# Output projections and the first dense chunks of a decoder trunk: two weight chunks begun together, four row tiles in PSUM banks 4 to 7, their last two inner slices at the end

## The chip, the cores and the metric

The kernel runs on one core of one Trainium2 chip. The metric is the time of the whole program in microseconds of device time; lower is better. Times in this text are microseconds unless marked otherwise.

TensorE (PE) multiplies into PSUM, which has eight banks; VectorE (DVE) and ScalarE (ACT) read PSUM and SBUF, GpSimd (POOL) reads SBUF; SyncE (SP) issues the weight DMAs. Each engine works through its own list in order and meets the others at semaphores.

## What is computed

One inference step of a decoder trunk of two layers, in fp32, for a prompt of 256 tokens and 8 sample tokens with the same weights (264 token columns together), D_MODEL = 1024:

```
for i in range(DEPTH):
    mix = mixer(rms_norm(x, norm_mix_g[i]), ...)      # z = xn @ w_in; conv, retention, gates
                                                      # m = sigmoid(ga)*a + sigmoid(gr)*r;  mix = m @ w_o
    x = x + mix
    hn = rms_norm(x, norm_ffn_g[i])
    if i % 2 == 0:
        f = swiglu(hn, w_dense_gu, w_dense_down)      # layer 0: dense, inner width 3584
    else:
        f = moe(hn, w_router, w_exp_gu, w_exp_down)   # layer 1: top 2 of 8 experts
    x = x + f
    gate = sigmoid(rms_norm(x, norm_ple_g[i]) @ w_ple_gate[i])
    x = x + gate * (p[i] @ w_ple[i])
return rms_norm(x, norm_final_g), conv states, retention states
```

The change touches m @ w_o in both layers and the first columns of hn @ w_dense_gu in layer 0.

## The kernel before

**Tiles and chunks.** Activations lie transposed: a row tile is 128 features by 264 tokens, and x has eight of them. Weights stream in chunks of 128 by 2048 fp32 (1 MB). SP loads chunk c into `raw`, a ring of six. ACT rounds it to `whi` (`cast`, L994) and DVE writes the remainder to `wlo` (`cast`, L1537), both rings of three. A product is three matmuls, whi x hi, whi x lo, wlo x hi (`three`, L2135). A chunk of the output projection or the dense up projection holds eight inner slices (k = 0 to 7) of two row tiles, so a row tile is 24 matmuls and a chunk 48.

**Order and waits.** ACT may cast chunk c once chunk c - 2 has begun on PE (`chunk_begun`, given by the first matmul of a chunk). PE waits for `lo_done` of its chunk (`ready`). A finished row tile gives `tile_ready`; the engine that reads it out gives `tile_taken`. Tiles are numbered through the program; tile p goes to bank p % 3 and waits until tile p - 3 is taken, unless `IN_BANK` and `FREE_AFTER` (L400 to L409) name another bank and another tile to wait for (`free`, L2126). `chunk` (L2143) runs its row tiles one after the other, all eight slices of each; with `each` the first tile waits before every slice for that slice's right operand.

**Output projection ("o", four chunks, eight row tiles, both layers).** Its right operand is m, in frt, split into high and low parts tile by tile; the low parts are DVE's L1734, and the tiles of x that the result is added to are DVE's L1763. The first chunk is run by `chunk_late` (L2160): six slices of tile 0, six of tile 1, then the last two slices of tile 0 and of tile 1; its two tiles are in banks 4 and 5. The other three chunks go through `chunk`. DVE's list in this stage is, for i = 0 to 3:

```
for i in range(4):
    cast(b["o"] + i + AHEAD)                     # AHEAD = 2
    if i > 0: split_x(..., 2 * i - 1)            # xl of tile 2i-1
    for j in (2 * i, 2 * i + 1): ...             # L1763: x[:, j] += PSUM, gives tile_taken
    split_x(..., 2 * i)                          # xl of tile 2i
```

ACT's list runs alike: cast of chunk o+i+2, then the high parts of x (`split_x`, L1001) for tiles 2i-1 and 2i, each waiting for DVE's add. POOL sums the squares of the x tiles into `sacc` as they come (`squares`, L585).

**Dense block, first half ("gu0", layer 0).** Right behind o. Its first chunk takes xh and xl as right operands, slice k waiting for xl of x tile k. After the first three slices of its second tile come two matmuls (`stat`, "L2282") that sum `sacc` over the partitions; from them ACT takes a root (L1019) and DVE makes rstd (`recip`, L1559), with which DVE multiplies every gu0 tile as it drains it (`take`, L1568, in rows L1571). ACT's list here: cast gu0+2, root, wait for the drains of tiles 0 and 1, Silu of both, cast gu0+3. DVE's: cast gu0+2, rstd, drain tiles 0 and 1, cast gu0+3, drain tiles 2 and 3, cast gu0+4 and so on.

**Behind o in layer 1** come the first tile of the w_ple product, then matmuls with an identity that turn xh and xl into token rows (`token_hi`, `token_lo`, L1832 and L1838), and the routing. The third `token_lo` writes the bank of o's last tile and waits for `tile_taken` of all o tiles.

**The input projection of layer 1** already starts with `two_late` (L2182): two chunks together, six slices of each of four tiles, stat, then the last two slices of all four.

Of the kernel before, what the change touches and what calls it, by code (L numbers as in the profile page):

```python
# [44 lines left out]
DEPTH = 2  # L45
# [5 lines left out]
RAW, CAST = 6, 3  # L51
# [99 lines left out]
def program(nc, A, O):  # L151
# [4 lines left out]
    with es:  # L156
# [247 lines left out]
        IN_BANK.update({TB[l]["o"] + i: 4 + i for l in range(DEPTH) for i in range(2)})  # L404
# [4 lines left out]
        FREE_AFTER.update({TB[l]["o"] + i: None for l in range(DEPTH) for i in range(2)})  # L409
# [1709 lines left out]
        def _(pe):  # L2119
            mm = nc.tensor.matmul  # L2120

            def ready(c, turns=0):

                pe.wait_ge(lo_done, RAW * turns + c + 1)
# [35 lines left out]
            def chunk_late(c, p, each, norm, ah, al):  # L2160

                ready(c)
                outs = [free(p), free(p + 1)]

                def some(n, ks):

                    for k in ks:
                        if n == 0:
                            pe.wait_ge(each[0], each[1][k])
                        at = k * 256 + n * 128  # L2170
                        ins = three(outs[n], whi[:, c % CAST, at:at + 128], wlo[:, c % CAST, at:at + 128],
                                    ah[:, k, :], al[:, k, :], k == 0, k == 7, n == 0 and k == 0)
                    return ins

                some(0, range(6))
                some(1, range(6))
                some(0, (6, 7)).then_inc(tile_ready, 1)
                if norm is not None:
                    stat(norm)
                some(1, (6, 7)).then_inc(tile_ready, 1)  # L2180

            def two_late(c, p, each, norm):  # L2182

                outs = [free(p + n) for n in range(4)]

                def some(n, ks, begins=False):

                    cc, h = c + n // 2, n % 2
                    for k in ks:
                        if n == 0:  # L2190
                            pe.wait_ge(each[0], each[1][k])
                        at = k * 256 + h * 128
                        ins = three(outs[n], whi[:, cc % CAST, at:at + 128], wlo[:, cc % CAST, at:at + 128],
                                    xht[:, k, :], xlt[:, k, :], k == 0, k == 7, begins and k == ks[0])
                    return ins

                ready(c)
                some(0, range(6), True)
                some(1, range(6))
                ready(c + 1)  # L2200
                some(2, range(6))
                some(3, range(6))
                stat(norm)
                some(0, (6, 7)).then_inc(tile_ready, 1)
                some(1, (6, 7)).then_inc(tile_ready, 1)
                some(2, (6, 7), True).then_inc(tile_ready, 1)
                some(3, (6, 7)).then_inc(tile_ready, 1)
# [101 lines left out]
            for l in range(DEPTH):  # L2309
# [14 lines left out]
                else:  # L2324
                    two_late(b["in"], t["in"], x_split(24), 3)
# [94 lines left out]
                chunk_late(b["o"], t["o"], (m_lo, [8 * l + k + 1 for k in range(8)]), None, frt[:, 8:16, :], frt[:, 16:24, :])  # L2420
                for i in range(1, 4):
                    chunk(b["o"] + i, t["o"] + 2 * i, 8, 2, frt[:, 8:16, :], frt[:, 16:24, :])
                if l == 0:
                    for hf in range(2):
                        c0, t0 = b["ffn"] + 22 * hf, t[f"gu{hf}"]
                        if hf == 0:
                            chunk(c0, t0, 8, 2, xht, xlt, each=x_split(8), norm=1, at_tile=1, at_k=2)
                        else:
                            chunk(c0, t0, 8, 2, xht, xlt)
                        chunk(c0 + 1, t0 + 2, 8, 2, xht, xlt)  # L2430
# [59 lines left out]
```

## Time and profile before

| | |
|---|---|
| median of 3 runs | 1721.24 us (1718.92 to 1721.98) |
| the profiled execution | 1718.33 us, span 1716.5 us |
| PE busy | 1697.8 us (99% of the span) |
| DVE busy | 1398.7 us (81%) |
| ACT busy | 1084.9 us (63%) |
| POOL busy | 188.8 us (11%) |
| DMA | 494.92 MB, mean 288 GB/s |
| mean granted TensorE clock | 0.998 |

The profile is of one execution; its span runs from the first to the last instruction. A matmul's length in a row (0.28 us for 264 columns) holds its way through the array; in a row of matmuls they start every 0.12 us. The time in brackets stands with an instruction in front of which its engine was idle, with the engine and line that ended the idle time.

### The profile page before, as it was taken

Reading aid. Unit: us, or ns where it says so; the run is one execution under the profiler, and the core shown is the slowest. Engines: PE = TensorE matmul, PEld = TensorE weight load, DVE = VectorE, ACT = ScalarE, POOL = GpSimd, SP = SyncE. Lnnn points to the kernel's source line nnn. Section 1 sums busy time; section 2 is a strip of 40 time slices with the busy share of each in tenths; the row PEclk is TensorE's granted clock in tenths of the full one; section 3 lists DMA queues with packets and bytes.
Section 4 is the critical chain, followed back from the end, with each engine's and each line's share of the span. In section 5 each row is a group of like instructions: output and inputs, shape, how many; then the busy total and the mean of one; then the engine's idle time right before and its main releaser. Section 6 shows DMA issues by size and latency. Waiting matters only on the chain.

```text
span 1716.5 us, 27369 instructions
## 1 busy us (share of the span) xinstructions
PE 1697.8 (99%) x10380; PEld 1517.3 (88%) x10380; DVE 1398.7 (81%) x1271; ACT 1084.9 (63%) x922; POOL 188.8 (11%) x166
## 2 busy tenths in 40 slices
PE   9999999999999999999999999999999999999997
PEld 8999999999999999878888888888888888888787
DVE  7876776566697867799898989898888988989898
ACT  5345444434563454677777777777777777777766
POOL 2112410000221122430000000000000000000002
PEclk9999999999999999999999999999999999999999
DMA  9755555655565554599999999999999999999990
GB/s 305 253 185 166 172 173 151 208 179 150 196 197 196 174 178 153 186 356 389 373 393 393 363 392 376 370 394 369 375 388 370 379 390 353 394 384 342 383 358 26
DMA packets 281536, 494.92 MB, mean 288 GB/s; under 512 B 8472, under 2 KB 127464, under 8 KB 281460
## 3 DMA queue, kind: packets, MB, share of 16 engines
q1 hardware_dynamic: 275104, 473.03, 77.2%
q0 software_dynamic: 6144, 20.67, 4.5%
q8 instruction: 55, 0.90, 0.2%
q10 hardware_dynamic: 212, 0.14, 0.0%
q14 instruction: 21, 0.17, 0.0%
HBM read 481.58 MB, written 12.23 MB: 288 GB/s over the span
## 4 chain that ended last, share of the span: by engine, by line
PE 88%; DVE 7%; ACT 2%; DMA 2%; issue 1%; DVEq 0%; POOL 0%; SPq 0%; ACTq 0%
PE PS L1920 11%; PE PS L1924 11%; PE PS L1923 11%; PE PS L2137 11%; PE PS L2140 10%; PE PS L2141 10%; PE PS L1940 6%; PE PS L1944 6%; PE PS L1943 6%; DVE wlo L1540 3%; DMA raw<-in_w_exp_gu 2%; ACT whi L999 2%; PE PS L1958 1%; PE PS L2381 1%; DVE xl L1547 1%
## 5 line engine op out<-in xcount | busy, mean ns | idle before, releaser
L1540 DVE TENSOR_TENSOR wlo<-raw,whi 128x2048 fp32r<-128x2048 f32 x450 | 1039.6, 2314 | 220.6 <-ACT whi L999 215.9
L999 ACT ACTIVATE whi<-raw 128x2048 fp32r<-128x2048 f32 x449 | 860.2, 1918 | 363.8 <-PE PS L2137 158.2
L1920 PE MATMUL PS<-whi,xh 128*128 128x512 f32 x896 | 355.1, 396 | 2.2 <-DVE wlo L1540 1.6
L1924 PE MATMUL PS<-whi,xl 128*128 128x512 f32 x896 | 349.7, 390 | 0.0
L1923 PE MATMUL PS<-wlo,xh 128*128 128x512 f32 x896 | 349.1, 390 | 0.0
L2137 PE MATMUL PS<-xh,whi 128*128 128x264 f32 x1168 | 334.4, 286 | 1.4 <-DVE z L1571 1.0
L2140 PE MATMUL PS<-xl,whi 128*128 128x264 f32 x1168 | 331.0, 283 | 0.0
L2141 PE MATMUL PS<-xh,wlo 128*128 128x264 f32 x1168 | 330.8, 283 | 0.0
L2137 PEld LDWEIGHTS PS<-xh,whi 128*128 128x128 f32 x1168 | 220.0, 188 | 2.8 <-DVE xl L1547 0.9
L2140 PEld LDWEIGHTS PS<-xl,whi 128*128 128x128 f32 x1168 | 220.1, 188 | 0.2
L2141 PEld LDWEIGHTS PS<-xh,wlo 128*128 128x128 f32 x1168 | 219.0, 188 | 0.0
L1920 PEld LDWEIGHTS PS<-whi,xh 128*128 128x128 f32 x896 | 168.4, 188 | 38.3 <-DVE wlo L1540 4.7
L1924 PEld LDWEIGHTS PS<-whi,xl 128*128 128x128 f32 x896 | 168.2, 188 | 35.9
L1923 PEld LDWEIGHTS PS<-wlo,xh 128*128 128x128 f32 x896 | 168.4, 188 | 33.0
L1940 PE MATMUL PS<-whi,fr 128*128 128x512 f32 x448 | 175.4, 391 | 0.1
L1944 PE MATMUL PS<-whi,fr 128*128 128x512 f32 x448 | 174.4, 389 | 0.0
L1943 PE MATMUL PS<-wlo,fr 128*128 128x512 f32 x448 | 174.4, 389 | 0.0
L2137 PE MATMUL PS<-fr,whi 128*128 128x264 f32 x480 | 137.4, 286 | 1.2 <-DVE fr L1734 1.2
L2141 PE MATMUL PS<-fr,wlo 128*128 128x264 f32 x480 | 136.4, 284 | 0.0
L2140 PE MATMUL PS<-fr,whi 128*128 128x264 f32 x480 | 135.9, 283 | 0.0
L1940 PEld LDWEIGHTS PS<-whi,fr 128*128 128x128 f32 x448 | 84.1, 188 | 18.1 <-DVE wlo L1540 0.9
L1944 PEld LDWEIGHTS PS<-whi,fr 128*128 128x128 f32 x448 | 84.1, 188 | 17.5
(322 smaller groups left out, 1674.8 us busy)
## 6 DMA issues: line engine op xcount, KB each, us to landing
raw<-in_w_exp_gu SPq DMA_DIRECT2D x224, 1024.0 KB, 7.3
raw<-in_w_exp_down SPq DMA_DIRECT2D x112, 1024.0 KB, 6.7
raw<-in_w_in SPq DMA_DIRECT2D x43, 1024.0 KB, 5.5
raw<-in_w_dense_gu SPq DMA_DIRECT2D x28, 1024.0 KB, 5.0
raw<-in_w_dense_down SPq DMA_DIRECT2D x16, 896.0 KB, 5.1
raw<-in_w_o SPq DMA_DIRECT2D x8, 1024.0 KB, 4.8
raw<-in_w_ple_gate SPq DMA_DIRECT2D x8, 1024.0 KB, 7.0
scr<-in_state_ret POOLq DMA_DIRECT2D x8, 512.0 KB, 4.8
```

The costliest lines, as they stand in the source:

```text
L999: nc.scalar.activation(whi[:, c % CAST, :], raw[:, c % RAW, :], ACT.Copy).then_inc(hi_done, 1)
L1540: v.tensor_tensor(wlo[:, c % CAST, :], raw[:, c % RAW, :], whi[:, c % CAST, :].bitcast(F32), ALU.subtract).then_inc(lo_done, 1)
L1547: v.scalar_tensor_tensor(lo[:, j, :], x[:, j, :], vec[:, GAIN[norm] + j:GAIN[norm] + j + 1], hi[:, j, :].bitcast(F32), ALU.mult, ALU.subtr ...
L1920: ins = mm(PS[:, bank, :], gh[:, 128 * kk:128 * kk + 128], wh, start=kk == 0, stop=False)
L1923: mm(PS[:, bank, :], gh[:, 128 * kk:128 * kk + 128], wl, start=False, stop=False)
L1924: ins = mm(PS[:, bank, :], gl[:, 128 * kk:128 * kk + 128], wh, start=False, stop=kk == 7)
L1940: ins = mm(PS[:, h, :], ah, wh, start=first and kk == 0, stop=False)
L1943: mm(PS[:, h, :], ah, wl, start=False, stop=False)
L1944: ins = mm(PS[:, h, :], al, wh, start=False, stop=last and kk == 3)
L2137: ins = mm(out, wh, ah, start=first, stop=False)
L2140: mm(out, wh, al, start=False, stop=False)
L2141: return mm(out, wl, ah, start=False, stop=last)
```

## The change

`chunk_late` goes. `two_late` gets the operands and a place for stat as arguments and is used in three more places: the first two chunks of o in both layers, and the first two chunks of gu0. In each, PE does slices 0 to 5 of tiles 0, 1 (first chunk), 2 and 3 (second chunk), and then slices 6 and 7 of tiles 0, 1, 2, 3. The second chunk's `chunk_begun` is given by the first of its last slices. The four tiles lie in banks 4 to 7. In gu0, stat comes after the six slices of the third tile instead of within the second. Tiles 4 to 6 of o wait only for what was before o to be taken; gu0's tiles 0 to 3 wait for o's tiles 0 to 3. Tile 7 of o and gu0's tiles from 4 on keep the general rule. The lists of DVE, ACT, POOL and SP are unchanged.

```diff
-        IN_BANK.update({TB[l]["o"] + i: 4 + i for l in range(DEPTH) for i in range(2)})
+        GU0 = TB[0]["gu0"]
+        IN_BANK.update({TB[l]["o"] + i: 4 + i for l in range(DEPTH) for i in range(4)})
+        IN_BANK.update({GU0 + i: 4 + i for i in range(4)})
...
-        FREE_AFTER.update({TB[l]["o"] + i: None for l in range(DEPTH) for i in range(2)})
+        for l in range(DEPTH):
+            FREE_AFTER.update({TB[l]["o"] + i: None for i in range(4)})
+            FREE_AFTER.update({TB[l]["o"] + i: TB[l]["o"] for i in range(4, 7)})
+        FREE_AFTER.update({GU0 + i: TB[0]["o"] + i + 1 for i in range(4)})
...
-            def two_late(c, p, each, norm):
+            def two_late(c, p, each, norm, ah, al, after=4):
...
-                ready(c)
-                some(0, range(6), True)
-                some(1, range(6))
-                ready(c + 1)
-                some(2, range(6))
-                some(3, range(6))
-                stat(norm)
+                for n in range(4):
+                    if n % 2 == 0:
+                        ready(c + n // 2)
+                    some(n, range(6), n == 0)
+                    if norm is not None and n + 1 == after:
+                        stat(norm)
                 some(0, (6, 7)).then_inc(tile_ready, 1)
                 some(1, (6, 7)).then_inc(tile_ready, 1)
                 some(2, (6, 7), True).then_inc(tile_ready, 1)
...
-                    two_late(b["in"], t["in"], x_split(24), 3)
+                    two_late(b["in"], t["in"], x_split(24), 3, xht, xlt)
...
-                chunk_late(b["o"], t["o"], (m_lo, [8 * l + k + 1 for k in range(8)]), None, frt[:, 8:16, :], frt[:, 16:24, :])
-                for i in range(1, 4):
+                two_late(b["o"], t["o"], (m_lo, [8 * l + k + 1 for k in range(8)]), None, frt[:, 8:16, :], frt[:, 16:24, :])
+                for i in range(2, 4):
                     chunk(b["o"] + i, t["o"] + 2 * i, 8, 2, frt[:, 8:16, :], frt[:, 16:24, :])
...
                         if hf == 0:
-                            chunk(c0, t0, 8, 2, xht, xlt, each=x_split(8), norm=1, at_tile=1, at_k=2)
+                            two_late(c0, t0, x_split(8), 1, xht, xlt, after=3)
                         else:
                             chunk(c0, t0, 8, 2, xht, xlt)
-                        chunk(c0 + 1, t0 + 2, 8, 2, xht, xlt)
+                            chunk(c0 + 1, t0 + 2, 8, 2, xht, xlt)
```

## Rows read from the trace of the kernel before

**Rows 1.** The page, part 1: busy time of each engine and share of the span.
```profile
PE 1697.8 (99%) x10380; PEld 1517.3 (88%) x10380; DVE 1398.7 (81%) x1271; ACT 1084.9 (63%) x922; POOL 188.8 (11%) x166
```

**Rows 2.** Waits of PE, 180 to 235 us: total, times, longest.
```profile
PE PS L2137 <- DVE fr L1734: 0.6, 2, 0.3
PE PS L2137 <- DVE z L1571: 0.5, 1, 0.5
PE PS L2137 <- DVE xl L1547: 0.4, 2, 0.3
```

**Rows 3.** Timeline of PE: start, length, instruction. Starts of o's tile 7 and gu0.
```profile
213.12 0.29 PE L2137 MATMUL PS<-fr,whi 128*128 128x264 f32 x1
...
216.02 0.29 PE L2137 MATMUL PS<-xh,whi 128*128 128x264 f32 x1
```

**Rows 4.** Timeline of PE, tile 0 of o, layer 0, slices 3 to 5.
```profile
193.02 0.28 PE L2141 MATMUL PS<-fr,wlo 128*128 128x264 f32 x1
...
194.52 0.39 PE L2137 MATMUL PS<-fr,whi 128*128 128x264 f32 x1 [0.27 <-DVE fr L1734]
```

**Rows 5.** Timeline of PE, gu0, layer 0: slices 6 and 7 of tile 0, stat, tile 3.
```profile
218.06 0.29 PE L2141 MATMUL PS<-xh,wlo 128*128 128x264 f32 x1
...
219.41 0.39 PE L2137 MATMUL PS<-xh,whi 128*128 128x264 f32 x1 [0.27 <-DVE xl L1547]
...
220.97 0.61 PE L2282 MATMUL PS<-sacc,con 128*128 128x264 f32 x2
...
226.80 0.39 PE L2137 MATMUL PS<-xh,whi 128*128 128x264 f32 x1 [0.48 <-DVE z L1571]
```

**Rows 6.** Timeline of DVE, 178 to 240 us: adds, a split, a cast, rstd, drains.
```profile
199.58 0.89 DVE L1763 TENSOR_TENSOR x<-PS,x 128x264 f32<-128x264 f32 x2
...
205.01 0.89 DVE L1763 TENSOR_TENSOR x<-PS,x 128x264 f32<-128x264 f32 x2
...
210.95 0.89 DVE L1763 TENSOR_TENSOR x<-PS,x 128x264 f32<-128x264 f32 x2
...
215.98 0.99 DVE L1547 SCALAR_TENSOR_TENSOR xl<-x,vec,xh 128x264 fp32r<-128x264 f32 x1
...
220.16 2.66 DVE L1540 TENSOR_TENSOR wlo<-raw,whi 128x2048 fp32r<-128x2048 f32 x1 [0.81 <-ACT whi L999]
222.75 0.42 DVE L1562 TENSOR_SCALAR nwt<-PS 128x264 f32<-128x264 f32 x1
...
226.31 0.77 DVE L1571 TENSOR_TENSOR z<-PS,rstd 128x264 f32<-128x264 f32 x2
...
231.81 0.77 DVE L1571 TENSOR_TENSOR z<-PS,rstd 128x264 f32<-128x264 f32 x2
...
235.82 0.43 DVE L1571 TENSOR_TENSOR z<-PS,rstd 128x264 f32<-128x264 f32 x1 [0.70 <-PE PS L2141]
```

**Rows 7.** Timeline of ACT, 178 to 240 us: a cast, the root, a cast.
```profile
200.46 1.90 ACT L999 ACTIVATE whi<-raw 128x2048 fp32r<-128x2048 f32 x1
...
221.62 0.48 ACT L1019 ACTIVATE sq_root<-PS,epsb 128x264 f32<-128x264 f32 x1 [0.18 <-PE PS L2282]
...
227.67 1.90 ACT L999 ACTIVATE whi<-raw 128x2048 fp32r<-128x2048 f32 x1
```

**Rows 8.** Timeline, end of o in layer 1: DVE's last adds, PE's low-part tokens.
```profile
696.15 0.89 DVE L1763 TENSOR_TENSOR x<-PS,x 128x264 f32<-128x264 f32 x2
...
696.50 1.12 PE L1828 MATMUL PS<-idr,xl 128*88 128x128 f32 x12
```

**Rows 9.** Timeline of DVE, head of layer 1's input projection: drains of tiles 0, 1 and 2, 3.
```profile
507.50 0.77 DVE L1571 TENSOR_TENSOR z<-PS,rstd 128x264 f32<-128x264 f32 x2
...
510.38 0.77 DVE L1571 TENSOR_TENSOR z<-PS,rstd 128x264 f32<-128x264 f32 x2
```

**Rows 10.** Timeline of POOL: sums of squares, one beside a cast of DVE, the last one.
```profile
213.93 2.75 POOL L595 TENSOR_TENSOR sacc<-sacc,sq 128x264 f32<-128x264 f32 x1
...
219.92 0.75 POOL L595 TENSOR_TENSOR sacc<-sacc,sq 128x264 f32<-128x264 f32 x1
```

**Rows 11.** Windows: PE, PEld, DVE, ACT, POOL busy, granted clock, DMA share, GB/s.
```profile
1700.00:1716.00 16.00, 7.87 (x64) 7.05 (x62) 10.05 (x21) 9.12 (x20) 3.57 (x5) 0.83 0.19 68
```

More of the change, by code:

```diff
@@ L2158, in chunk @@
                             stat(norm)
-            def chunk_late(c, p, each, norm, ah, al):
-                ready(c)
[L2163 to L2175, printed above, removed]
-                some(1, range(6))
-                some(0, (6, 7)).then_inc(tile_ready, 1)
-                if norm is not None:
-                    stat(norm)
-                some(1, (6, 7)).then_inc(tile_ready, 1)
-            def two_late(c, p, each, norm):
+            def two_late(c, p, each, norm, ah, al, after=4):
                 outs = [free(p + n) for n in range(4)]
@@ L2193, in some @@
                         ins = three(outs[n], whi[:, cc % CAST, at:at + 128], wlo[:, cc % CAST, at:at + 128],
-                                    xht[:, k, :], xlt[:, k, :], k == 0, k == 7, begins and k == ks[0])
+                                    ah[:, k, :], al[:, k, :], k == 0, k == 7, begins and k == ks[0])
                     return ins
-                ready(c)
-                some(0, range(6), True)
-                some(1, range(6))
-                ready(c + 1)
-                some(2, range(6))
-                some(3, range(6))
-                stat(norm)
+                for n in range(4):
[4 more added lines that the diff above has]
+                        stat(norm)
                 some(0, (6, 7)).then_inc(tile_ready, 1)
```

## The prediction, made blind

> **What bounds the kernel now.** I read the page first, for who is busy: TensorE is busy 99% of the span [rows 1]. So a change helps only if it removes a moment in which PE stands still, and hurts if it adds one. Next the waits of PE in the stretch that the diff touches in layer 0, from the output projection ("o", eight tiles) to the first tiles of the dense block ("gu0"): five waits, 1.5 us together by its rounded sums [rows 2]. They understate the loss, because a restarted PE runs its first matmul with a 0.1 us larger step. The timeline of PE gives it from start to start. Two starts 24 matmuls (one tile) apart differ by 2.90 us, 0.1208 us for a matmul, and tile 7 of o ends when gu0 begins, at 216.02 [rows 3]. Before that, slices 4 and 5 of tile 0 of o wait for parts of m: from 193.02 to 194.52 lie four steps, 0.48 us at full pace and 1.50 in fact [rows 4]; with a last refill of 0.1 that is 1.12 us lost. In gu0, slices 6 and 7 of tile 0 wait for xl in the same way: four steps from 218.06 to 219.41, 0.87 too many, 0.98 with the refill. The two "stat" matmuls at 220.97 cost 0.45 us with the refill behind them, and stay. Tile 3 is due 39 matmuls behind them, at 226.15, and starts at 226.80, since tile 0 isn't drained: 0.75 us with the refill [rows 5].
>
> Then the two engines that drain and split, because every new order on PE changes when they get their tiles. In o, DVE's adds into x (L1763), two tiles a time, start at 199.58, 205.01, 210.95, with a cast between each [rows 6]. These are not paced by PE: tiles 2 and 4 are complete long before. They close a ring: add of tile 2i, ACT's split of x, ACT's cast behind it (at 200.46, 0.88 after the add), DVE's cast of the same chunk, DVE's split, next add: 5.43 us round, 5.94 us where the split takes 0.99 us [rows 6, 7]. PE needs 5.80 us for two tiles. So the ring is as slow as PE and never catches up what it is delayed by. This decides the case.
>
> **Part 1: o, both layers.** Before, tiles 0 and 1 are finished first. Counting from 191.69 (216.02 less eight tiles and 1.12), tile 0 ends after 42 matmuls, at 197.88. After, its last two slices come behind six slices of all four tiles: 78 matmuls, 202.23. The slices that wait today (4 and 5) are still the first thing PE does, so their 1.12 us is not removed. DVE can read a tile some 0.28 us after its last slot (0.28 is a matmul's own length at 193.02; the nearest drain: gu0's tile 5 starts at 232.71, as below, and fills 2.90, so it is complete at 235.61, and its drain starts at 235.82 [rows 6], which makes 0.2 the lower bound). Tile 0 then starts its add at 202.51 instead of 199.58. Of the 4.35 us by which it ends later, 1.42 were covered, since DVE was still casting, and **2.93 us** go into the ring. Behind that add stand, in order, ACT's split 0, the cast of chunk 3 on ACT and DVE (which also waits for "chunk 1 begun", now at 203), and all later ones. Tile 4's add moves from 210.95 to 213.88 and ends at 214.31. PE's tile 7 shares tile 4's bank and is due at 213.12 (216.02 less 2.90): it starts at 214.37, and with the refill **1.36 us** are lost where nothing was. Casts: chunk 3 is ready at 207.5 and due at 210.2, so it costs nothing. gu0 begins at 217.38.
>
> **Part 2: gu0, layer 0.** The split of x tile 5 ends at 215.98 + 0.99 = 216.97 now [rows 6] and at 219.90 with the shift; slice 5 of tile 0 is due at 219.19, so 0.77 and a refill, 0.88 us, are lost. Slices 6 and 7 come last and no longer wait. Stat follows three tiles of six slices: 217.38 + 0.88 + 54 x 0.1208 = 224.78. ACT's root starts 0.65 after stat (220.97 to 221.62) and takes 0.48; DVE's rstd steps then start at 225.96 (its cast in front, begun at 220.16, ends with the shift at 225.7). From there rows give distances: 3.56 to the drain of tile 0 (222.75 to 226.31), so 229.52; and 5.50 to the drain of tile 2 (226.31 to 231.81), in which lie the Silu and the cast of chunk gu0+3, first on ACT, then on DVE [rows 6, 7]: 235.02, ended 235.45. Tile 3 has a bank of its own now, which takes its 0.75 us away. But tile 5 goes to the ring bank and by the unchanged rule waits for tile 2's drain. It is due 66 matmuls and 0.45 after stat, at 233.2, and starts at 235.51. With the refill its first full step is at 235.62. Before it was 226.80 + 0.11 + 48 x 0.1208 = 232.71. Layer 0 loses **2.91 us** in all, which holds the 1.36 and 0.88 and what is saved (0.98 and 0.75). From there PE paces DVE again, and the loss is passed on whole.
>
> **Part 3: the end of layer 1's o.** The same ring, 1.36 us at tile 7. Then the four identity matmuls of the third low-part token block, which start near 697.14 (third of three groups from 696.50), wait until tile 7's add has ended: 696.15 + 0.89 = 697.04, hardly any slack [rows 8]. With the shift that is 699.97: PE stands again, and the layer loses **2.89 us** in all. What follows (token copies, routing) hangs on PE, and POOL's last sum, 2.9 later, is still ahead of its use.
>
> **Unknown sizes.** The existing head of layer 1's input projection already runs in this order. There tile 2 is drained 2.88 us after tile 0, since no Silu lies between [rows 9]: with that value layer 0 would lose only some 0.5 us (233.2 against 232.71). I keep 5.50, since ACT's order in gu0 is the one near 227 and isn't changed. A split takes 0.49 or 0.99 us; over three of them the ring can be 1 us shorter or longer. With the drain latency I bound each layer by 1.9 and 3.9 us, layer 0 by 0.5 with the short drain.
>
> **Sum.** 2.91 + 2.89 = 5.8 us on the profiled execution: 1718.33 (span 1716.5 and 1.8 around it) to 1724.1. The median shown, 1721.24, is 2.9 above that execution, so I give 1721.24 + 5.8 = 1727.0.
>
> **Rivals.** (a) The faster one: the ring catches up, DVE's adds of tiles 4 to 7 fall back to PE's pace before tile 7 is due. Place: between 202.5 and 213.1 in o. Then 0.98 + 0.75 are saved and nothing is paid: 1719.5. It decides for faster from the point where the shift is under 1.7 us at tile 4 (no wait at tile 7) and under some 0.5 us at gu0's tile 2. Against it: the ring has no idle time to give back. 0.05. (b) One layer pays in full, the other hardly, as with the short drain: +2.9 to 3.4, 1724.4. 0.12. (c) POOL: its sum of squares beside a DVE cast takes 2.75 us instead of 0.75 to 0.92; its last one starts at 219.92, 0.24 before the cast [rows 6, 10]. If the phase slips it ends with the cast, stat comes some 1.8 us later and so does tile 5: 1728.8. 0.08. The Trainium skill (GPSIMD Engine Reference, Specifications) says that GpSimd shares its SBUF interfaces with VectorE instructions that have two SBUF inputs, as the cast has; the stretched row agrees, and which case holds here the page doesn't say. (d) The clock: it is granted at 0.83 in the last 16 us, where PE is busy 7.87 [rows 11]. Of the two levels, 2.4 and 1.2 GHz, a mean of 0.83 is 5.4 us at the lower, a loss of 2.7 us if such a drop came once after the new 2.2 us wait: 1729.7. 0.04. The Trainium skill (TensorE: Matmul & The Clock Gate, Part 1) holds that an idle PE is throttled, which speaks against adding waits; no row here shows it for one of 2 us. (e) The change doesn't bite (drains bound elsewhere, no difference): 1721. 0.03. Forecast: 0.68.
>
> **Chances and range.** About 0.2% (3.4 us) is what a measurement of this kernel can tell from no change. Faster by more would need 3.4 us of gain, more than all that the change can save: 0.02. Slower holds the forecast but for its lower edge, with (c) and (d): 0.78. Same takes (a), (b), (e): 0.20. The forecast's own bounds are 1725.0 and 1729.0; reaching to (b) and (d) and a scatter of 1.5 us gives 1721.5 to 1731.
>
> **What would show it.** In the profile after: PE waiting on DVE's L1763 for about 1.2 us ahead of tile 7 of o in both layers; a wait on xl of 0.7 us at gu0's slice 5, none at 6 and 7; one of about 2.2 us on DVE's drain ahead of gu0's tile 5, and none ahead of tile 3; about 1.4 us on L1763 ahead of the token matmuls; first adds of o some 2.9 us later against the start of o, with equal distances behind. A first add under 1 us later, or adds 5.4 apart throughout, would break the forecast.

## The result, and the profile after

The changed kernel takes **1726.4 us** (median of 6 runs, 1725.89 to 1729.39) against 1720.37 for the kernel before on the same chip (6 runs, 1718.04 to 1722.65): a ratio of 1.0035, 95% interval 1.0025 to 1.0045, so 6.0 us slower, 4.3 to 7.7. The forecast was 5.8 us more, and 1727.0. The profiled execution of after took 1726.67 (span 1724.9, mean granted clock 0.995) beside 1718.33 for the one of before (span 1716.5, clock 0.998).

Line numbers in after are 5 higher than in the rows of before: the add is L1768, the split L1552, the drain L1576, the matmuls L2142 to L2146. Busy time, part 1 of the page:

```profile
PE 1701.0 (99%) x10380; PEld 1521.5 (88%) x10380; DVE 1399.1 (81%) x1271; ACT 1084.6 (63%) x922; POOL 190.3 (11%) x166
```

The instruction counts are those of [rows 1], and DVE, ACT and POOL are as busy as before. The loss must be PE's waits and, for the 3.2 us by which PE is busier with the same matmuls, its clock. The waits of PE from 180 to 240 us (engine, tile and line, what it waited for: total, times, longest), to be held against [rows 2]:

```profile
PE PS L2142 <- DVE z L1576: 2.0, 1, 2.0
PE PS L2142 <- DVE x L1768: 1.1, 1, 1.1
PE PS L2142 <- DVE fr L1739: 0.6, 2, 0.3
PE PS L2142 <- DVE xl L1552: 0.6, 1, 0.6
```

The two waits on `fr` are the same as before, so what PE waited for at the head of o is still paid. New are one wait on an add (L1768), one of 2.0 where a drain cost 0.5, and a single one on a split. Timeline of PE (start, length, instruction, idle time before it and its releaser): tile 7 of o, slice 5 of gu0's tile 0, and gu0's tile 5. The last one begins the stretch shown in full further below.

```profile
215.06 0.39 PE L2142 MATMUL PS<-fr,whi 128*128 128x264 f32 x1 [1.11 <-DVE x L1768]
...
220.63 0.39 PE L2142 MATMUL PS<-xh,whi 128*128 128x264 f32 x1 [0.60 <-DVE xl L1552]
...
236.18 0.39 PE L2142 MATMUL PS<-xh,whi 128*128 128x264 f32 x1 [1.98 <-DVE z L1576]
```

Timeline of DVE: the first two adds of o, which are apart now, then the adds of tiles 2 and 3, 4 and 5, 6 and 7, and the drains of gu0's tiles 0 and 1, 2 and 3.

```profile
203.11 0.43 DVE L1768 TENSOR_TENSOR x<-PS,x 128x264 f32<-128x264 f32 x1 [2.81 <-PE PS L2146]
203.91 0.43 DVE L1768 TENSOR_TENSOR x<-PS,x 128x264 f32<-128x264 f32 x1 [0.36 <-PE PS L2146]
...
208.67 0.89 DVE L1768 TENSOR_TENSOR x<-PS,x 128x264 f32<-128x264 f32 x2
...
214.59 0.89 DVE L1768 TENSOR_TENSOR x<-PS,x 128x264 f32<-128x264 f32 x2
...
220.50 0.89 DVE L1768 TENSOR_TENSOR x<-PS,x 128x264 f32<-128x264 f32 x2
...
230.20 0.77 DVE L1576 TENSOR_TENSOR z<-PS,rstd 128x264 f32<-128x264 f32 x2
...
235.70 0.76 DVE L1576 TENSOR_TENSOR z<-PS,rstd 128x264 f32<-128x264 f32 x2
```

This execution is 0.63 us late before anything of the change begins (the first matmul of the retention output starts at 180.59, in before at 179.96), so 0.63 comes off each of these times. The first add is then at 202.48, where 202.51 was worked out; against [rows 6] it is 2.90 later. The adds behind it are at 208.04, 213.96 and 219.87: gaps of 5.56, 5.92 and 5.91 us. The ring gives nothing back.

Layer 1, waits of PE from 660 to 720 us, and the timeline of the matmuls concerned, tile 7 of o and the third low-part token block, which in [rows 8] ran without a wait:

```profile
PE PS L1833 <- DVE x L1768: 1.2, 1, 1.2
PE PS L2142 <- DVE x L1768: 1.1, 1, 1.1
```

```profile
700.26 0.39 PE L2142 MATMUL PS<-fr,whi 128*128 128x264 f32 x1 [1.11 <-DVE x L1768]
...
706.64 0.53 PE L1833 MATMUL PS<-idr,xl 128*88 128x128 f32 x4 [1.24 <-DVE x L1768]
```

**Where the 8.3 us between the two profiled executions lie.** Lined up by the count of matmuls, after is 0.63 us late up to o in layer 0 and 5.11 late behind the head of gu0 (4.48 lost in between). It is 6.66 late ahead of layer 1's o (1.5 lost between 622 and 626), 9.56 late behind it (2.90 lost), and 8.34 late at the end: near 1600 us, in the experts, which the change doesn't touch, the kernel before loses 1.3 us and after doesn't. Layer 1's share is the forecast one (2.89). Layer 0's is 1.6 above the forecast 2.91. That excess is in the clock. Timeline of PE behind the last wait, and windows from 225 to 250 us (columns as in [rows 11]; the clock stands before the last two):

```profile
236.41 0.28 PE L2145 MATMUL PS<-xl,whi 128*128 128x264 f32 x1
236.53 0.28 PE L2146 MATMUL PS<-xh,wlo 128*128 128x264 f32 x1
...
237.01 0.42 PE L2146 MATMUL PS<-xh,wlo 128*128 128x264 f32 x1
237.23 0.42 PE L2142 MATMUL PS<-xh,whi 128*128 128x264 f32 x1
...
240.36 0.28 PE L2142 MATMUL PS<-xh,whi 128*128 128x264 f32 x1
240.48 0.29 PE L2145 MATMUL PS<-xl,whi 128*128 128x264 f32 x1
```

```profile
225.00:236.00 11.00, 9.20 (x74) 8.85 (x72) 8.16 (x10) 6.06 (x6) 0.00 (x0) 1.00 0.29 95
236.00:237.00 1.00, 0.82 (x5) 0.82 (x6) 1.00 (x3) 0.00 (x0) 0.00 (x0) 0.87 0.01 2
237.00:240.00 3.00, 3.00 (x15) 3.00 (x15) 2.00 (x2) 0.00 (x0) 0.00 (x0) 0.50 0.96 322
240.00:250.00 10.00, 10.00 (x84) 10.00 (x83) 5.83 (x7) 4.90 (x4) 0.00 (x0) 0.99 0.61 197
```

From 236.8 to 240.1 matmuls start every 0.22 us instead of every 0.12: 0.50 of the full clock, the lower of the two levels (1.2 of 2.4 GHz). Some 15 matmuls lose 0.10 each, 1.5 us. The same thing happens in this execution at 620 to 630 (clock 0.74 from 620 to 625, 0.91 from 625 to 630), with PE busy throughout and nothing of the change near; of the 13 traces of this case, 8 have such a stretch there. The trace of the kernel before has none between its first 8 and its last 6 us. So a stretch at the lower level is not by itself a mark of the change, and the execution compared with is one without any.

### The profile page after: what moved, and what is told of

It is laid out like the page before. It is cut to its first block, busy times and chain, and to the rows that moved or that the text cites. A ratio compares the mean times of both kernels' runs of the same rounds, so it can differ in the third digit from the quotient of the medians.

```text
span 1724.9 us, 27368 instructions
## 1 busy us (share of the span) xinstructions
PE 1701.0 (99%) x10380; PEld 1521.5 (88%) x10380; DVE 1399.1 (81%) x1271; ACT 1084.6 (63%) x922; POOL 190.3 (11%) x166
## 4 chain that ended last, share of the span: by engine, by line
PE 89%; DVE 7%; ACT 2%; issue 2%; DMA 0%; DVEq 0%; ACTq 0%
PE PS L1925 12%; PE PS L1929 12%; PE PS L1928 11%; PE PS L2142 10%; PE PS L2145 10%; PE PS L2146 10%; PE PS L1945 6%; PE PS L1949 6%; PE PS L1948 6%; DVE wlo L1545 3%; ACT whi L1004 2%; PE PS L1963 1%; PE PS L2363 1%; DVE xl L1552 1%; DVE z L1576 0%
## 5 line engine op out<-in xcount | busy, mean ns | idle before, releaser
L2142 PE MATMUL PS<-xh,whi 128*128 128x264 f32 x1168 | 336.0, 288 | 3.1 <-DVE z L1576 2.5
L2146 PE MATMUL PS<-xh,wlo 128*128 128x264 f32 x1168 | 332.3, 285 | 0.0
L2142 PEld LDWEIGHTS PS<-xh,whi 128*128 128x128 f32 x1168 | 221.5, 190 | 4.3 <-DVE z L1576 2.2
L2146 PEld LDWEIGHTS PS<-xh,wlo 128*128 128x128 f32 x1168 | 220.5, 189 | 0.0
L2142 PE MATMUL PS<-fr,whi 128*128 128x264 f32 x480 | 137.6, 287 | 3.4 <-DVE x L1768 2.2
L2146 PE MATMUL PS<-fr,wlo 128*128 128x264 f32 x480 | 136.4, 284 | 0.0
```

Of the source, the lines that this page charges most:

```text
L2142: ins = mm(out, wh, ah, start=first, stop=False)
L2146: return mm(out, wl, ah, start=False, stop=last)
```

## The experiments

The yardstick is a length within one execution, free of what came earlier: in layer 0 from the first matmul of the retention output to the first of gu0's tile 6 (before: 55.66 us), in layer 1 from the same matmul to the first expert's first "up" matmul (before: 55.84). "L0 +2.9" means 2.9 us longer than before. Ratios are of whole times. The lengths are read from one execution of each kernel. The cuts of code below are against after, unless another kernel is named; `...` marks lines or arguments left out.

| kernel | ratio, 95% interval | L0 | L1 |
|---|---|---|---|
| after | 1.0035, 1.0025 to 1.0045 | +4.48 (1.5 of it clock) | +2.90 |
| o alone | 1.0033, 1.0023 to 1.0044 | +2.96 | +2.87 |
| gu0 alone | 1.0013, 1.0004 to 1.0022 | +0.65 | -0.01 |
| tile 7 in bank 7 | 1.0072, 1.0058 to 1.0086 | +8.30 (flawed) | +4.40 (1.5 clock) |
| the same, waits one by one | 1.0053, 1.0037 to 1.0068 | +4.51 (1.5 clock) | +4.42 (1.5 clock) |
| late add in the old order | 1.0063, 1.0047 to 1.0078 | +5.07 | +6.13 |
| ring opened | 1.0013, 1.0004 to 1.0022 | +1.27 | +1.21 |
| cut at slice 4 in o | 1.0003, 0.9993 to 1.0012 | +0.36 | +0.25 |
| drains first in gu0 | 1.0026, 1.0016 to 1.0037 | +0.73 | +2.83 |
| fill in the wait | 1.0034, 1.0021 to 1.0046 | +2.92 | +2.83 |
| cut, open ring, drains first | 0.9983, 0.9973 to 0.9992 | -2.68 | -0.54 |
| cut, open ring, gu0 as before | 0.9990, 0.9980 to 1.0000 | -0.46 | -0.56 |

### Which half of the change costs: o alone, gu0 alone

```diff
-        IN_BANK.update({GU0 + i: 4 + i for i in range(4)})
-        FREE_AFTER.update({GU0 + i: TB[0]["o"] + i + 1 for i in range(4)})
...
-                            two_late(c0, t0, x_split(8), 1, xht, xlt, after=3)
+                            chunk(c0, t0, 8, 2, xht, xlt, each=x_split(8), norm=1, at_tile=1, at_k=2)
+                        chunk(c0 + 1, t0 + 2, 8, 2, xht, xlt)
```

> Only the output projections (both layers) run two chunks together in banks 4 to 7; gu0 is left as in the kernel before. Theory (the first add into x comes 2.9 us later, and the ring of add, ACT cast, DVE cast passes that on undiminished): 2.93 us lost in layer 0 and 2.89 in layer 1, +5.8 us or a ratio near 1.0034, the same as the whole change; in the trace PE waits about 1.1 us on the add ahead of o's tile 7 in both layers, slices 5, 6 and 7 of gu0's tile 0 wait for xl, and tile 3 of gu0 is reached 2.9 us later than before. Rival (the loss in layer 0 is made by the new order in gu0, its wait ahead of tile 5): only layer 1's 2.9 us and the 1.4 us at tile 7 of layer 0, minus nothing: +4.3 or less.

**Measured:** 1726.77 us beside 1719.63, L0 +2.96, L1 +2.87. Waits of PE in layer 0:

```profile
PE PS L2139 <- DVE xl L1549: 1.7, 3, 0.9
PE PS L2139 <- DVE x L1765: 1.1, 1, 1.1
```

The whole loss is there without gu0's new order, 5.8 us by the two lengths. The late adds of o are enough to make it. With gu0's new order on top, the list of waits is another (one split and a drain instead of three splits and the old drain) and the sum in layer 0 comes out the same; why is seen when the drain is moved, below.

```diff
-                two_late(b["o"], t["o"], (m_lo, [8 * l + k + 1 for k in range(8)]), None, ...)
+                chunk_late(b["o"], t["o"], (m_lo, [8 * l + k + 1 for k in range(8)]), None, ...)
```

> Only gu0 runs two chunks together in banks 4 to 7; the output projections are left as in the kernel before. Theory: the adds come as before, so slices 5 to 7 never wait (0.98 saved) and tile 3 doesn't (0.75 saved), but stat lies a tile later and tile 5 waits for the drain of tile 2 behind the Silu and a cast: stat at 222.5, tile 5 at 233.4 against 232.7, +0.7 us in all, a ratio of 1.0004, with a wait near 1.6 us ahead of tile 5. Rival (gu0's order is what costs): +2.9 us, 1.0017. Should the clock fall to its lower level after the wait ahead of tile 5, 1.6 us more in that execution.

**Measured:** 1722.59 us beside 1719.63, L0 +0.65, L1 unchanged. The one wait is gu0's tile 5 on the drain of tile 2:

```profile
PE PS L2140 <- DVE z L1574: 2.0, 1, 2.0
```

The three waits that go (two on splits, one on a drain; 1.73 us with their refills) pay for most of the new one. The ratio asks for 2.2 us, 0.7 to 3.8; the length shows 0.65, and its mean granted clock over all runs (0.9954 beside 0.9961) can hold the rest, which isn't shown.

### Is it the ring? A late add in the old order, and an opened ring

If the ring carries any delay undiminished, delaying o's first add alone must do what the change does. This is the kernel before with o's tiles 0 to 3 in banks 4 to 7, as in after, and one wait ahead of the first add (cut against before; the lines on banks are left out):

```diff
+                    else:
+                        dve.wait_ge(tile_ready, t["o"] + 4)
```

> PE's order of the kernel before, o's tiles 0 to 3 in banks 4 to 7 as in the change, and DVE starting its first add only when tile 3 is complete: the cause alone and larger, with neither the new order of matmuls nor gu0's banks. Tile 3 is complete at 204.7 on the time line of the kernel before, so the first add comes 5.1 us later instead of 2.9. Theory: both layers are longer by that, less the slack at their ends (0.0 to 0.5 us): +5.1 in layer 0 and +5.0 in layer 1, ratio 1.0058, plus what the clock takes behind waits of over 3 us. Rival (the ring has play and absorbs part; what costs is the order on PE): under +2 us a layer, ratio under 1.0023.

**Measured:** 1730.17 us beside 1720.14. The adds come at 204.51, 209.95, 215.88 and 221.79, 5.44, 5.93 and 5.91 apart. Against before and lined up, the first is 5.08 late, the last 5.05, and L0 is +5.07: the ring gives nothing back. PE meets it in a single wait, at tile 7, in both layers:

```profile
216.35 0.59 PE L2141 MATMUL PS<-fr,whi 128*128 128x264 f32 x1 [3.18 <-DVE x L1767]
```

```profile
216.00:222.00 6.00, 5.65 (x26) 5.65 (x27) 4.54 (x6) 2.73 (x3) 4.90 (x4) 0.51 0.54 175
```

Behind that wait the clock is at its lower level for 23 matmuls, which makes PE some 2.3 us later, and the waits on splits that gu0 had don't come any more. So PE's own slowness and the ring ask for nearly the same 5 us here, and it is the times of the adds that show the ring by itself. In layer 1 the adds are 4.9 late and 26 slow matmuls follow the wait: L1 is +6.13, some 1.1 above the 5.0 expected.

Now after with the ring opened: ACT casts the next chunk's high part one split earlier, so that this cast, and DVE's cast of the same chunk, no longer wait for DVE's next add.

```diff
+                cast(b["o"] + AHEAD)
                 for i in range(4):
-                    cast(b["o"] + i + AHEAD)
...
-                    split_x(NORM_OF["ffn", l], range(max(2 * i - 1, 0), 2 * i + 1))
+                    split_x(NORM_OF["ffn", l], (max(2 * i - 1, 0),))
+                    if i < 3:
+                        cast(b["o"] + i + 1 + AHEAD)
+                    if i > 0:
+                        split_x(NORM_OF["ffn", l], (2 * i,))
```

> The changed kernel with ACT's list in o changed: the cast of each chunk stands one split earlier (split 1, cast gu0, split 2, and so on), so that it no longer waits for DVE's next add; nothing is left out. The ring is open and catches up. By the rows: adds of tiles 4 and 5 from 212.6 (213.9 in the change, 211.0 before), of tiles 6 and 7 from 217.3; no wait ahead of tile 7, none at slice 5, 0.7 us lost in layer 0 at the drain of tile 2, 0.2 to 0.4 in layer 1. Theory: +1.0 us, ratio 1.0006. Rival (PE's order itself costs, whatever the adds do): 1.0030 or more.

**Measured:** 1723.04 us beside 1720.14, L0 +1.27, L1 +1.21. Tile 7 waits 0.2 us instead of 1.1; the 2.0 us ahead of gu0's tile 5 are still there. The first add is as late as in after, but the later ones catch up. DVE in layer 0, and POOL beside it:

```profile
211.63 0.89 DVE L1772 TENSOR_TENSOR x<-PS,x 128x264 f32<-128x264 f32 x2
...
213.11 2.85 DVE L1549 TENSOR_TENSOR wlo<-raw,whi 128x2048 fp32r<-128x2048 f32 x1
215.88 0.85 DVE L1556 SCALAR_TENSOR_TENSOR xl<-x,vec,xh 128x264 fp32r<-128x264 f32 x1
216.66 0.89 DVE L1772 TENSOR_TENSOR x<-PS,x 128x264 f32<-128x264 f32 x2
...
221.79 0.89 DVE L1772 TENSOR_TENSOR x<-PS,x 128x264 f32<-128x264 f32 x2
```

```profile
212.90 0.91 POOL L600 TENSOR_TENSOR sacc<-sacc,sq 128x264 f32<-128x264 f32 x1
213.88 2.56 POOL L599 TENSOR_TENSOR sq<-x 128x264 f32<-128x264 f32 x1
```

Rounds of 5.03 and 5.13 us stand against 5.92 and 5.91. That the ring is what carries the delay is shown by both runs: leave it closed and delay the add further, and all of it arrives at the last add; open it, and of 2.9 us at the first add 1.2 to 1.3 are left at the last. The size was missed: a round of about 4.7 us was expected, +0.7 in layer 0 and 0.2 to 0.4 in layer 1. The cast now begins while POOL's sum is running and takes 2.85 us instead of 2.29, and the split behind it takes 0.85 instead of 0.49. The Trainium skill (GPSIMD Engine Reference, Key points) says that GpSimd shares its SBUF interfaces with VectorE and names contention with VectorE instructions that have two SBUF inputs. The two rows agree; the page gives no price, and here it is 0.6 us on DVE, and 1.9 on POOL's squares (2.56, without company 0.63).

### Is it the bank of tile 7?

The rival to the ring at this place: PE waits at tile 7 only because it shares a bank with tile 4. Tile 7 goes to bank 7, whose tile 3 was taken long ago.

```diff
+        IN_BANK.update({TB[l]["o"] + 7: 7 for l in range(DEPTH)})
...
-        FREE_AFTER.update({GU0 + i: TB[0]["o"] + i + 1 for i in range(4)})
+        FREE_AFTER.update({TB[l]["o"] + 7: TB[l]["o"] + 4 for l in range(DEPTH)})
+        FREE_AFTER.update({GU0 + i: TB[0]["o"] + (i + 1 if i < 3 else 8) for i in range(4)})
```

> The changed kernel, with o's tile 7 in bank 7 (free as soon as tile 3 is added) instead of the bank of tile 4, in both layers. It takes PE's new 1.1 us wait ahead of tile 7 away and leaves the adds where they are. Theory (the ring of adds sets the end, the bank is only where PE meets it first): nothing is gained, the wait moves to slice 5 of gu0's tile 0 in layer 0 (2.0 instead of 0.6 us) and to the token matmuls in layer 1 (2.6 instead of 1.2 us); ratio to the kernel before 1.0035 as for the change. Rival (the bank conflict is the cause of its share): 2 x 1.36 us are gained, ratio 1.0019.

**Measured:** 1733.68 us beside 1719.63, more than either theory had, for a reason of its own in layer 0. gu0's tile 3 now shares a bank with o's tile 7, and `two_late` does the waits for all four of its banks ahead of its first matmul, so gu0 began only behind tile 7's add:

```profile
223.08 0.56 PE L2144 MATMUL PS<-xh,whi 128*128 128x264 f32 x1 [4.92 <-DVE x L1770]
```

Layer 1 is free of this flaw: no wait at tile 7, and 2.6 us at the tokens instead of 1.2. The next kernel asks for each bank just ahead of its tile:

```diff
-                outs = [free(p + n) for n in range(4)]
+                outs = []
...
                 for n in range(4):
                     if n % 2 == 0:
                         ready(c + n // 2)
+                    outs.append(free(p + n))
```

> The changed kernel with o's tile 7 in bank 7, as before, but gu0's four tiles now wait for their banks one by one, each ahead of its first matmul, instead of all four ahead of the first (the trial before this one made PE wait 4.9 us for tile 7's add there, which was an effect of its own). Theory: PE's 1.1 us wait ahead of tile 7 goes, and comes back whole at slice 5 of gu0's tile 0 (about 2.0 instead of 0.6 us) and, in layer 1, ahead of the token matmuls (2.6 instead of 1.2, as the layer-1 half of that trial already had). Apart from stretches at the lower clock, the way from o's slice 5 to gu0's tile 6 is 2.9 us longer than in the kernel before, as with the change, ratio 1.0033 and up. Rival (the shared bank is the cause of 1.36 us a layer): 1.5 us longer, ratio 1.0019.

**Measured:** 1729.6 us beside 1720.14. Waits of PE in layer 0, then in layer 1:

```profile
PE PS L2144 <- DVE xl L1554: 2.0, 1, 2.0
PE PS L2144 <- DVE z L1578: 2.0, 1, 2.0
```

```profile
PE PS L1835 <- DVE x L1770: 2.6, 1, 2.6
```

The wait at tile 7 is gone and comes back in full at the next thing that the ring releases: 0.6 grows to 2.0 at gu0's slice 5, 1.2 to 2.6 at the tokens. The bank only chose where PE stood. The kernel is slower than after, since the waits at gu0's tile 5 and at the tokens were each followed by some 15 matmuls at the lower level, 1.5 us: L0 +4.51 and L1 +4.42, of which +2.95 and +2.9 are the ring's.

### When the first add comes: the cut at slice 4

After with four slices first and four last in o (gu0 keeps six and two). Tile 0 is then complete after 60 matmuls instead of 78.

```diff
-                some(0, (6, 7)).then_inc(tile_ready, 1)
+                some(0, range(cut, 8)).then_inc(tile_ready, 1)
...
+                two_late(b["o"], ..., cut=4)
```

> The changed kernel with o's four tiles cut after four slices instead of six (slices 0 to 3 of tiles 0 to 3, then 4 to 7 of each); gu0 keeps six. Tile 0 is then complete after 60 matmuls, at 198.94 on the time line of the kernel before instead of 202.23, before DVE is free for it, and slices 4 and 5 no longer wait for m (1.12 us a layer). Theory: the first add is where it was before the change (199.6), the second 0.6 later, the ring is 0.2 us late instead of 2.9; PE is 1.12 us early and gives it back at slice 5 of gu0 and at the drain of tile 2, and in layer 1 at the token matmuls. Sum +0.1 in layer 0, +0.2 in layer 1: ratio 1.0002 (1.0000 to 1.0010). Rival (two chunks together cost by themselves): 1.0030.

**Measured:** 1720.76 us beside 1721.03, L0 +0.36, L1 +0.25. The head's two waits on `fr` are gone too, since slices 4 and 5 now come later. The first add is at 199.67, the adds of tiles 4 and 5 at 211.43:

```profile
199.67 0.43 DVE L1768 TENSOR_TENSOR x<-PS,x 128x264 f32<-128x264 f32 x1
200.75 0.43 DVE L1768 TENSOR_TENSOR x<-PS,x 128x264 f32<-128x264 f32 x1 [0.65 <-PE PS L2146]
...
211.43 0.89 DVE L1768 TENSOR_TENSOR x<-PS,x 128x264 f32<-128x264 f32 x2
```

The same reordering, with its first add near the old time, costs nothing that can be measured. It gains nothing either. gu0 begins 1.06 us earlier than in before, counted from the retention output, but the ring is 0.5 late: by stat 0.8 of the gain is gone, and gu0's own order costs the 0.65 that it costs alone.

### The wait at gu0's tile 5, and the clock

The drain of tiles 2 and 3 stands behind a cast. Here DVE takes all four tiles ahead of it (first time only):

```diff
-                cast(c + 1 + AHEAD, turns)
+                if not first:
+                    cast(c + 1 + AHEAD, turns)
...
+                if first:
+                    cast(c + 1 + AHEAD, turns)
```

> The changed kernel, with DVE draining gu0's tiles 2 and 3 before its cast of chunk gu0+3 instead of behind it. Theory: tile 5 no longer waits (2.0 us and a refill gone), layer 0 then loses 0.6 us instead of 2.9, layer 1 keeps its 2.9: +3.5 us, ratio 1.0020; and since PE isn't idle there the granted clock stays at 1.00 where the changed kernel's trace shows 0.50 for 3.3 us behind that wait, which is worth another 1.6 us in executions that have it (ratio down to 1.0011). Rival (PE meets the same delay at the next tile or cast): ratio 1.0035 unchanged.

**Measured:** 1724.68 us beside 1719.63; no wait ahead of tile 5, no low clock behind it, L0 +0.73 (+0.6 expected), L1 +2.83. DVE:

```profile
234.37 1.45 DVE L1579 TENSOR_TENSOR z<-PS,rstd 128x264 f32<-128x264 f32 x4
```

So the drain's place is worth 2.2 us, with the adds of o as late as in after. This wait is not the ring's. In gu0 alone, where the adds are in time, it is just as long (2.0), and from the first stat matmul to tile 5 lie 10.72 us in after (225.46 to 236.18) and 10.71 in gu0 alone (223.24 to 233.95). Stat in after, then stat and tile 5 in gu0 alone:

```profile
225.46 0.61 PE L2264 MATMUL PS<-sacc,con 128*128 128x264 f32 x2
```

```profile
223.24 0.61 PE L2284 MATMUL PS<-sacc,con 128*128 128x264 f32 x2
...
233.95 0.39 PE L2140 MATMUL PS<-xh,whi 128*128 128x264 f32 x1 [1.98 <-DVE z L1574]
```

The chain of root, rstd, drains, Silu and casts takes its time whenever stat comes. Layer 0's loss is therefore a sum: 1.36 and 0.88 us that the late adds cost at tile 7 and slice 5, less the 0.98 and 0.75 that gu0's new order saves, plus some 2.4 at tile 5. That it equals the delay of the first add is chance, and not the ring's doing; in o alone and in layer 1 it is the ring's. Together the lengths say +3.6, the ratio 4.5 (2.8 to 6.4).

The other one fills that wait: 16 matmuls that nothing needs, into a bank that is free, ahead of tile 4, so that PE reaches tile 5 when its bank is free.

```diff
                             two_late(c0, t0, x_split(8), 1, xht, xlt, after=3)
+                            pe.wait_ge(tile_taken, GU0 + 2)
+                            for i in range(16):
+                                mm(PS[:, 3, 0:T], whi[:, (c0 + 1) % CAST, 0:128], xht[:, 0, :], start=True, stop=True)
```

> The changed kernel with 16 matmuls into an unused bank put ahead of gu0's tile 4 (1.93 us of PE work that nothing needs), which fills the wait ahead of tile 5. Theory: tile 5 starts where it did (2.9 us later than in the kernel before), for the work lies in the wait; PE isn't idle there, and the stretch at 0.50 of the clock behind it doesn't come: the profile shows 1.00 from 225 to 250 us. Where the changed kernel has that stretch it is 1.5 us shorter, so the ratio is 1.0030 to 1.0035. Rival (the lower clock has nothing to do with the wait): the same ratio as the change, with such a stretch here as often. Should the added work not be hidden: +1.9 us more, 1.0046.

**Measured:** 1726.37 us beside 1720.14. Tile 5 starts 55.58 us after the first matmul of the retention output, in after 55.59, and the clock stays at 1.00:

```profile
236.00:240.00 4.00, 3.94 (x32) 3.73 (x32) 3.62 (x6) 0.03 (x1) 0.00 (x0) 1.00 0.71 225
```

The low stretch is absent in this profile, L0 is +2.92 instead of +4.48, and the time over six runs is after's, 1.0034 against 1.0035. So this one stretch is not what makes the change slow; what it adds to the mean of many runs, these intervals can't resolve. Nor does a wait of 2.0 us bring it for sure. Behind the wait at gu0's tile 5 it came in after and with the banks asked for one by one; it did not come behind the same wait in gu0 alone, in the first bank 7 kernel, with the ring opened and with the cut at slice 4, nor behind the 2.0 us wait at slice 5.

### All three together, and without gu0

After with the cut, the open ring and the drains first; then after with the cut and the open ring, but gu0 and its drains as in the kernel before. Both are put together from the cuts of code above.

> All three repairs on the changed kernel: o cut after four slices, ACT's casts in o one split earlier (open ring), DVE draining gu0's tiles 2 and 3 before the cast of chunk gu0+3. Theory: no wait on an add ahead of o's tile 7, at slice 5 or at the token matmuls, none on m, none at gu0's tiles 3 to 5. Layer 0 2.5 us and layer 1 1.0 us shorter than in the kernel before (rounds of the open ring taken at the 5.1 us that its own trial showed): -3.5 us, ratio 0.9980, between 0.9973 and 0.9990. Rival (something else ends last at each place): 1.0000.

**Measured:** 1717.19 us beside 1721.03: faster than both kernels, 0.9983, some 3 us. PE has no wait at all from 180 to 245 us, L0 is -2.68 (-2.5 expected) and L1 -0.54 (-1.0 expected). The adds and drains in layer 0:

```profile
202.31 0.43 DVE L1775 TENSOR_TENSOR x<-PS,x 128x264 f32<-128x264 f32 x1
...
213.16 0.89 DVE L1775 TENSOR_TENSOR x<-PS,x 128x264 f32<-128x264 f32 x2
...
228.90 1.45 DVE L1583 TENSOR_TENSOR z<-PS,rstd 128x264 f32<-128x264 f32 x4
```

> The output projections with two chunks together, cut after four slices, and the open ring, but gu0 and DVE's list as in the kernel before. Theory: layer 1 is 1.0 us shorter as with all three repairs; in layer 0 the adds come early enough for slices 6 and 7 but for 0.5 us, and tile 3 of gu0 still waits for rstd and the drain of tile 0: 1.1 us shorter than before. -2.1 us, ratio 0.9988. Rival (gu0's four banks are worth nothing): the same time as with all three.

**Measured:** 1719.51 us beside 1721.03, 0.9990, an interval that reaches 1; L0 -0.46 where -1.1 was expected, L1 -0.56 where -1.0 was. gu0 in its old order still waits 1.1 us on splits and 0.5 on a drain, and DVE's stretched casts keep the ring from gaining what the head gave. The 2.2 us between the two kernels' L0 are what gu0's new order and the drains are worth once the adds are in time.

## Why the prediction was right

**The delay of the first add** (2.93 us predicted): right, 2.90 by the timelines, from a count of 78 matmuls for 42, 1.42 of it covered and a read latency of 0.28.

**The ring carries it whole**: right, and the step on which most of the loss rested, 1.36 and 0.88 us in layer 0 and all of layer 1's. Adds of tiles 4 and 6 were given for 213.88 and 219.83 and came at 213.96 and 219.87. The late add (5.08 in at the first add, 5.05 out at the last) and the open ring (2.9 in, 1.2 to 1.3 out) show it as cause.

**The stations in layer 0**, lined up: tile 7 started at 214.43 (214.37), 1.31 us after it was due, with the refill 1.4 (1.36); slice 5 waited 0.60 and lost about 0.9 (0.88), slices 6 and 7 nothing; stat at 224.83 (224.78); the drains at 229.57 and 235.07 (229.52 and 235.02); tile 5 at 235.55 (235.51). The wait at tile 3 was gone. The prediction has the wait at tile 5 as a term of its own, and rightly: it comes from gu0's order, not from the ring, as gu0 alone and the moved drain show. Of the two distances between drains, 2.88 and 5.50 us [rows 6, 9], the one taken (5.50) was measured: 230.20 to 235.70.

**Layer 1**: right, 2.90 measured for 2.89, paid at the same two places, 1.1 at tile 7 and 1.2 at the tokens.

**The rivals.** (a), the ring catches up, did not happen; it needs another order on ACT, and the open ring shows even then a rest of 1.2. Its price of 1719.5 was wrong besides. It took the 0.98 and 0.75 as saved and nothing as paid, but the wait at tile 5 hangs on stat: gu0 alone, with its adds in time, keeps it and is 0.65 longer, not 1.7 shorter. (b): both layers paid. (c): POOL's last sum took 0.75 us and started at 223.54, ahead of the cast at 223.78 by 0.24, the old phase to the hundredth:

```profile
223.54 0.75 POOL L600 TENSOR_TENSOR sacc<-sacc,sq 128x264 f32<-128x264 f32 x1
```

(d), the clock, came beside the forecast in the profiled execution, where I had it as a case of its own at 2.7 us. The mechanism was real and the size 1.5 us; 2.7 was read from the end of the kernel [rows 11], where PE is busy half the time. It gave the whole case no new answer: it does not come each time, and the runs of the unchanged kernel go from 0.994 to 0.998 in their mean granted clock, which points to such stretches there too, though its one trace has none. The Trainium skill (TensorE: Matmul & The Clock Gate, Part 1) holds that an idle PE is throttled; the 0.50 behind the 2.0 us wait agrees, the waits of the same length without it and the 0.74 at 620 to 625 with PE busy throughout do not follow from that alone.

**The sum.** 5.8 predicted, 5.8 by the lengths of o alone, 2.95 + 2.90 = 5.85 by those of after less the clock, 6.0 (4.3 to 7.7) by the ratio. The time of 1727.0 was 0.6 too high because its base was: the median of three runs, 1721.24, where six give 1720.37. What I left out is that two profiled executions can differ by more than the effect: these two by 8.3, where beside the 5.85 there are 1.5 from the low stretch in gu0, 0.6 ahead of the change and 1.5 near 620 us, less 1.3 in the experts.

## What to carry to other kernels

Before work is put off so that its inputs are in time, ask which engine waits for its *first result*. If that result enters a ring of engines (here add on DVE, split and cast on ACT, cast and split on DVE, next add) whose round is as long as the bound engine's own (5.9 and 5.8 us), every microsecond of delay arrives at its last result, and is lost wherever the bound engine stands ready for it. Work that is reordered to need the late results later can hide a part, as slices 6 and 7 of gu0 did. The idle time in front of it is the smaller number: here 2.9 us per layer stood against 1.7 us of waits removed in one of them.

Moving a bank only moved where such a delay was paid. Shorten the ring, or bring the first result back to its old time: the reordering was worth 3 us once both were done and the drains moved as well, and minus 6 without. And look at each wait by itself: the longest one in after, 2.0 us at tile 5, had nothing to do with the late adds.

Measure such effects within an execution, from a mark ahead of the change to one behind it, and let the whole times confirm them.

## What the runs showed of the hardware

**The lower clock level comes in short stretches.** Behind single waits of 2.6, 3.2 and 4.9 us it came each time (five cases), behind waits of 2.0 us in two cases of seven, and behind one of 2.1 in the kernel with the drains first (at 43 us, clock 0.50 from 44.0 to 46.5). A stretch holds some 15 matmuls at half pace in the common case, about 1.5 us lost, and 23 to 26 behind the waits of 3.2 and 4.9 us; little of it shows if PE would have waited again soon after (the late add in layer 0). It also comes where PE is busy throughout. In the 28 runs of the kernel before that stand beside the last three kernels, those with a mean granted clock of 0.998 took 1717.7 to 1718.3 us and those with 0.995 took 1721.4 to 1723.2, so much of the scatter between runs of one kernel, 0.2 to 0.3%, goes with it.

**When POOL's sums and DVE's casts meet, the later one waits.** After, layer 0, DVE's cast first and POOL's sum 0.15 us behind it:

```profile
211.48 2.29 DVE L1545 TENSOR_TENSOR wlo<-raw,whi 128x2048 fp32r<-128x2048 f32 x1 [1.24 <-ACT whi L1004]
```

```profile
211.63 2.74 POOL L600 TENSOR_TENSOR sacc<-sacc,sq 128x264 f32<-128x264 f32 x1
```

The cast keeps its 2.29 us, and the sum ends 0.60 after the cast does. With the ring opened it is the other way round: the cast at 213.11 begins while the sum of 212.90 is running and takes 0.56 longer, and the square begun at 213.88 ends 0.48 after the cast. So it cost DVE nothing to begin first and half a microsecond in each round to begin second. This is read from these rows; no run tested it by itself. The whole trace of before agrees on DVE's side: its 382 casts beside which POOL did nothing and its 29 casts that began ahead of POOL's instruction took 2.27 to 2.29 us, and every cast over 2.3 us had begun while an instruction of POOL was running, though not each cast begun so was longer.
